# The end of a group of experts in another order: results copied ahead of the last roundings, the last subtraction in two halves, results and final squares piece by piece

## What is computed

```
g_w, g_idx = lax.top_k(g_prob, 1)                  # one of 8 groups for each token
top_v, top_i = lax.top_k(e_sel, TOP_K)             # two of the 8 experts of that group
gate = (g_w * jax.nn.softmax(top_v, axis=-1)).reshape(-1)
def expert_block(args):
    xb, e = args
    return (jax.nn.silu(xb @ w1[e]) * (xb @ w3[e])) @ w2[e]
x = x + hier_moe(h, ...)
return rms_norm(x, final_norm)
```

## Time and profile before

| | |
|---|---|
| median of 3 runs | 1842.92 us (1842.17 to 1843.37) |
| the profiled execution | 1841.25 us, its span 1839.4 us |
| busy TensorE matmuls | 1741.4 us (95%) |
| busy VectorE | 1521.0 us (83%) |
| busy ScalarE | 1219.1 us (66%) |
| busy GpSimd | 132.4 us (7%) |
| read from HBM | 542.33 MB, 295 GB/s over the span |
| loop over the groups | from about 890 us to 1825 us of the span |
| mean granted clock of TensorE | 0.991 |

### The profile page before, as it was taken

The page is one execution under the profiler, slowest core; times in us unless marked ns, Lnnn a source line. Parts: engine busy times, 40 slices in busy tenths (PEclk is TensorE's granted clock), DMA queues, the critical chain, the costliest instruction groups (busy, mean ns, idle before and its releaser), DMA issues.

```text
span 1839.4 us, 26378 instructions
## 1 busy us (share of the span) xinstructions
PE 1741.4 (95%) x10394; PEld 1522.0 (83%) x10394; DVE 1521.0 (83%) x1284; ACT 1219.1 (66%) x947; POOL 132.4 (7%) x140
## 2 busy tenths in 40 slices
PE   6999999999999999999999999999999999999996
PEld 6987899989899989978877877778777777778775
DVE  4787665678565666678899999999999999999997
ACT  4465444343323335545688988889898898888985
POOL 1155000000000001441000000000000000000000
PEclk9999999999999999999999999999999999999999
DMA  6431254563344555227699999999999999999994
GB/s 248 187 130 70 110 199 171 196 246 141 138 172 176 199 197 217 95 80 295 260 429 426 428 429 429 428 420 429 428 428 428 430 429 428 428 428 428 430 428 174
DMA packets 40645, 544.13 MB, mean 296 GB/s; under 512 B 4624, under 2 KB 4752, under 8 KB 5904
## 3 DMA queue, kind: packets, MB, share of 16 engines
q1 hardware_dynamic: 40592, 543.39, 72.1%
HBM read 542.33 MB, written 1.05 MB: 295 GB/s over the span
## 4 chain that ended last, share of the span: by engine, by line
PE 59%; DMA 13%; issue 7%; ACT 6%; DVE 4%; POOL 1%; DVEq 0%; ACTq 0%; POOLq 0%; SPq 0%
PE psum L1394 17%; DMA ring<-in_w 13%; PE psum L984 12%; PE psum L834 7%; PE psum L994 6%; PE psum L1408 4%; ACT arena_r L1802 4%; PE psum L1423 2%; DVE ring_r L2309 2%; PE psum L877 2%; PE psum L1159 1%; PE psum L894 1%; PE psum L1332 1%; PE psum L1296 1%; PE psum L1456 1%
## 5 line engine op out<-in xcount | busy, mean ns | idle before, releaser
L2309 DVE TENSOR_TENSOR ring_r<-ring,arena_r 128x4096 fp32r<-128x4096 f32 x192 | 846.7, 4418 | 17.1 <-ACT arena_r L1802 13.1
L1802 ACT ACTIVATE arena_r<-ring 128x4096 fp32r<-128x4096 f32 x188 | 682.3, 3629 | 65.6 <-DMA ring<-in_w 63.7
L1394 PE MATMUL psum<-arena_r,stream_r 128*128 128x512 f32 x1024 | 410.8, 401 | 11.5 <-DVE stream_r L2398 9.2
L1394 PE MATMUL psum<-ring_r,stream_r 128*128 128x512 f32 x1024 | 403.2, 394 | 0.0
L1394 PEld LDWEIGHTS psum<-arena_r,stream_r 128*128 128x128 f32 x1024 | 194.9, 190 | 56.5 <-DVE ring_r L2309 11.3
L1592 ACT ACTIVATE arena_r<-ring 128x3072 fp32r<-128x3072 f32 x40 | 110.9, 2773 | 188.6 <-DMA ring<-in_ffn 188.6
L1394 PEld LDWEIGHTS psum<-ring_r,stream_r 128*128 128x128 f32 x1024 | 194.9, 190 | 39.1
L984 PE MATMUL psum<-arena_r 128*128 128x256 f32 x672 | 190.2, 283 | 0.0
L984 PE MATMUL psum<-stream_r,ring_r 128*128 128x256 f32 x672 | 190.1, 283 | 0.0
L984 PE MATMUL psum<-stream_r,arena_r 128*128 128x256 f32 x672 | 190.1, 283 | 0.0
L1423 PE MATMUL psum<-arena_r 128*128 128x512 f32 x512 | 161.1, 396 | 11.7 <-DVE arena_r L2457 10.8
(11 more groups left out here) (327 smaller groups left out, 2675.8 us busy)
## 6 DMA issues: line engine op xcount, KB each, us to landing
ring<-in_w SPq DMA_DIRECT2D x192, 2048.0 KB, 12.9
ring<-in_ffn SPq DMA_DIRECT2D x44, 1536.0 KB, 6.3
ring<-in_w_in SPq DMA_DIRECT2D x8, 2048.0 KB, 8.1
ring<-in_in_w SPq DMA_DIRECT2D x7, 2048.0 KB, 13.0
ring<-in_out_w SPq DMA_DIRECT2D x7, 2048.0 KB, 8.2
ring<-in_l_in SPq DMA_DIRECT2D x8, 1536.0 KB, 8.5
ring<-in_proj SPq DMA_DIRECT2D x2, 2048.0 KB, 8.5
ring<-in_misc SPq DMA_DIRECT2D x1, 1632.0 KB, 8.8
```

What stands on the lines that cost most here:

```text
L1394: last = mm(dst, xg[:, k, :], b[:, k * D_EXPERT:(k + 1) * D_EXPERT], start=(k == 0 and b is u_hi), stop=(k == KD - 1 and b is u_lo))
L1802: A(w_hi[u % HI_SLOTS], ring[:, MOE_SLOT[at], :], ACT.Copy).then_inc(m_hi, 1)
L2309: V.tensor_tensor(ring_r[MOE_SLOT[u % NM]][:, :], raw, w_hi[u % HI_SLOTS].bitcast(F32), ALU.subtract).then_inc(m_lo, 1)
```

## The change

Seven edits; the counters keep their meaning where nothing else is said.

- ScalarE: the result copies of units 18 and 19 go ahead of the roundings H(21) and H(22), and from there on each rounding comes one iteration later. The new order: H(20), copy 17, copy 18, H(21), silu 6, copy 19, H(22), round 6, silu 7, H(23), round 7, H(24), gathered tokens, H(25), H(26), y, H(27).
- VectorE: L(23) is cut into two halves of 2048 columns. The new order: L(22), subtract 6, multiply 7, first half of L(23), subtract 7, second half, L(24), L(25), gathered tokens, L(26), y, L(27).
- TensorE starts unit 23 on the first half (`m_lo_first`) and waits for the second one in its middle.
- y: each half is counted by itself (`m_y_lo` goes by two per group), and `send_back` waits before each piece for the half that it reads.
- After the last group the step on rank stands in front of the last `add_back`.
- Each of the last two squares waits for the pieces of its own token half (`m_scd` starts at 2 instead of 1, and the waits on it are one higher).
- The copy of rank, `moe_done` and GpSimd's wait on it are gone.

```diff
@@ the plan of the units
+        LATE = MOE.index(("w1", PER_GROUP - 1)) - 1
@@ TensorE, expert_out
-                pe.wait_ge(m_lo, n * NM + (u + 1))
+                if u == NM - 1:
+                    pe.wait_ge(m_lo_first, n + 1)
+                else:
+                    pe.wait_ge(m_lo, n * NM + (u + 1))
...
                 for j in range(NE):
+                    if u == NM - 1 and j == NE // 2:
+                        pe.wait_ge(m_lo, n * NM + NM)
@@ TensorE, send_back
-                pe.wait_ge(m_y_lo, n)
                 for i, (tc, h) in enumerate(RES):
+                    pe.wait_ge(m_y_lo, 2 * n + h)
@@ ScalarE, the loop over the units
-                        if kind != "w2":
-                            act.wait_ge(m_unit, n * NM + (u + 1))
-                            A(h_raw[:, e % 2, 0 if kind == "w1" else 1, :], psum[:, H1_BANK if kind == "w1" else H3_BANK, :],
-                              ACT.Copy).then_inc(m_raw, 1)
+                        if kind != "w2" and u <= LATE:
+                            raw(u)
...
-                        if u + HI_SLOTS < NM:
-                            split_hi(u + HI_SLOTS, n)
-                        elif u < NM - 1:
-                            with act.If(n + 1 < passes * N_GROUPS):
-                                split_hi(u + HI_SLOTS, n)
+                        if u in (LATE, LATE + 1):
+                            raw(u + 1)
+                        if u < LATE + 2:
+                            next_hi(u + HI_SLOTS)
+                        elif u > LATE + 2:
+                            next_hi(u + HI_SLOTS - 1)
...
-            square("last", lambda tc: (moe_done, 1))
+            for tc in range(NT):
+                act.wait_ge(m_scd, passes * (4 * N_GROUPS) + 2 * tc)
+                A(xn[:, tc, :], x[:, tc, :], ACT.Square, accum_out=ss[:, NORMS["last"], tc:tc + 1]).then_inc(squares, 1)
@@ VectorE
+            def split_lo_rows(i, done):
+
+                slot, at = MOE_SLOT[NM - 1], slice(i * SLOT // 2, (i + 1) * SLOT // 2)
+                V.tensor_tensor(ring_r[slot][:, at], ring[:, slot, at], w_hi[(NM - 1) % HI_SLOTS][:, at].bitcast(F32),
+                                ALU.subtract).then_inc(done, 1)
...
-                        if u + 3 < NM:
+                        if u + 3 < NM - 1:
                             split_lo(u + 3, n)
-                        else:
-                            with dve.If(n + 1 < passes * N_GROUPS):
-                                split_lo(u + 3, n)
                         if u in FOLD_AT:
...
+                        if u + 3 == NM - 1:
+                            dve.wait_ge(m_hi, n * NM + NM)
+                            split_lo_rows(0, m_lo_first)
                         if u in TURN_AT:
...
+                        if u + 3 == NM:
+                            split_lo_rows(1, m_lo)
+                        if u + 3 >= NM:
+                            with dve.If(n + 1 < passes * N_GROUPS):
+                                split_lo(u + 3, n)
...
-                        last = V.tensor_tensor(y_lo[:, at], psum[:, Y_BANK[i], :], y_hi[:, at].bitcast(F32), ALU.subtract)
-                    last.then_inc(m_y_lo, 1)
+                        V.tensor_tensor(y_lo[:, at], psum[:, Y_BANK[i], :], y_hi[:, at].bitcast(F32),
+                                        ALU.subtract).then_inc(m_y_lo, 1)
                 n = dve.snap(p * N_GROUPS + N_GROUPS)
-                add_back(n)
                 V.tensor_scalar(rank, rank, float(CAP), None, ALU.subtract).then_inc(scaled_ready, 1)
                 dve.wait_ge(scaled_ready, p + (1 + NT))
-            dve.wait_ge(m_scd, passes * (4 * N_GROUPS) + 1)
-            V.tensor_copy(last_rank, rank).then_inc(moe_done, 1)
+                add_back(n)
```

More of the change, by code:

```diff
@@ L401, in program @@
         gate8, rank8, rank = few(NT, 8), few(NT, 8), few(NT)
-        last_rank, most, passes_f = few(NT), few(1), few(1)
+        most, passes_f = few(1), few(1)
         psum = ctx.enter_context(nc.psum_tensor("psum", [P, 8, 512], F32))
@@ L440, in program @@
         m_gate_mm, m_sel_turned, m_selT, m_gate = sem("m_gate_mm"), sem("m_sel_turned"), sem("m_selT"), sem("m_gate")
-        m_hi, m_lo, m_unit, m_silu, m_h = sem("m_hi"), sem("m_lo"), sem("m_unit"), sem("m_silu"), sem("m_h")
+        m_hi, m_lo, m_lo_first, m_unit, m_silu, m_h = sem("m_hi"), sem("m_lo"), sem("m_lo_first"), sem("m_unit"), sem("m_silu"), sem("m_h")
         m_raw, m_fold, m_hT_hi, m_hT_lo = sem("m_raw"), sem("m_fold"), sem("m_hT_hi"), sem("m_hT_lo")
         m_y_hi, m_y_lo, m_sc, m_scd = sem("m_y_hi"), sem("m_y_lo"), sem("m_sc"), sem("m_scd")
-        moe_done, out_ready, out_sent = sem("moe_done"), sem("out_ready"), sem("out_sent")
+        out_ready, out_sent = sem("out_ready"), sem("out_sent")
         O = PsumOrder(tile_ready, act_drained, dve_drained)
@@ L1414, in expert_out @@
                 e = MOE[u][1]
-                pe.wait_ge(m_lo, n * NM + (u + 1))
+                if u == NM - 1:
+                    pe.wait_ge(m_lo_first, n + 1)
+                else:
+                    pe.wait_ge(m_lo, n * NM + (u + 1))
                 pe.wait_ge(m_hT_lo, n * PER_GROUP + (e + 2))
                 if e == 0:
-                    pe.wait_ge(m_scd, n * 4 + 1)
+                    pe.wait_ge(m_scd, n * 4 + 2)
                 u_hi, u_lo = w_hi[u % HI_SLOTS], ring_r[MOE_SLOT[u]]
                 for j in range(NE):
+                    if u == NM - 1 and j == NE // 2:
+                        pe.wait_ge(m_lo, n * NM + NM)
                     for b in (u_hi, u_lo):
@@ L1814, in _, with raw, next_hi @@
                     n = act.snap(p * N_GROUPS + g)
+                    def raw(u):
+                        kind, e = MOE[u]
+                        act.wait_ge(m_unit, n * NM + (u + 1))
+                        A(h_raw[:, e % 2, 0 if kind == "w1" else 1, :], psum[:, H1_BANK if kind == "w1" else H3_BANK, :],
+                          ACT.Copy).then_inc(m_raw, 1)
+                    def next_hi(u):
+                        if u < NM:
+                            split_hi(u, n)
+                        else:
+                            with act.If(n + 1 < passes * N_GROUPS):
+                                split_hi(u, n)
                     for u, (kind, e) in enumerate(MOE):
-                        if kind != "w2":
-                            act.wait_ge(m_unit, n * NM + (u + 1))
-                            A(h_raw[:, e % 2, 0 if kind == "w1" else 1, :], psum[:, H1_BANK if kind == "w1" else H3_BANK, :],
-                              ACT.Copy).then_inc(m_raw, 1)
+                        if kind != "w2" and u <= LATE:
+                            raw(u)
                         if u in FOLD_AT:
@@ L1838, in _ @@
                         A(y_hi[:, i * 512:(i + 1) * 512], psum[:, Y_BANK[i], :], ACT.Copy).then_inc(m_y_hi, 1)
-                    with act.If(n + 1 < passes * N_GROUPS):
-                        split_hi(NM - 1 + HI_SLOTS, n)
+                    next_hi(NM - 1 + HI_SLOTS)
                 n = act.snap(p * N_GROUPS + N_GROUPS)
@@ L2356, in _ @@
             V.engine_nop().then_inc(r_gate, 1)
-            V.engine_nop().then_inc(m_scd, 1)
+            V.engine_nop().then_inc(m_scd, 2)
+            V.engine_nop().then_inc(m_y_lo, 1)
             V.engine_nop().then_inc(m_sc, 4)
@@ L2588, in _ @@
             norm(5)
-            pool.wait_ge(moe_done, 1)
             norm("last")
```

## The result

| | before | changed |
|---|---|---|
| median | 1843.14 us (1842.17 to 1845.72, 4 runs) | 1861.49 us (1856.75 to 1867.03, 4 runs) |
| the profiled execution | 1841.25, span 1839.4 | 1859.95, span 1858.1 |
| groups apart (start of unit 0 of the next group) | 117.7 | 120.85 |
| mean granted clock | 0.991 | 0.982 |

The changed kernel takes 1.0102 times as long, interval 1.0087 to 1.0116: slower, as forecast, by 18.4 us instead of 11. The time lies 7.5 us above the forecast and 1.5 above the range.

A forecast was written before the change was run, and what follows sets the result against it. The DMA was taken to set the pace, three resources lying within 6%. Seven passages x 2.1 = 14.7 us later landing puts unit 23's end 13.5 later; less 2.2 in the tail, +11.3: 1854 us, range 1841 to 1860.

The forecast's parts named there:

- the row with a like wait: TensorE at each next group's start: 1.8 us of slower matmuls after 7 us of standstill, chosen between 0 and 3.5.
- the tail: Behind the last group's unit 23: send-back, rank step and squares start earlier, a gain taken as 2.2 us.
- the slow GpSimd step: Inverse root behind the second square: 1.39 us beside a VectorE multiply, median 0.551; kept, else the tail would gain 2.8.
- Rival D: Passages: H(23) isn't late because fold 7 runs sooner; both gains stand, 1.2+2.2, faster at 1839.5 us; chance 0.08.
- Rival C: Passages: lateness is absorbed in each group, the stall staying below VectorE's spare 2.8 us; not slower, 1840.7 us; chance 0.17.
- the larger of the two: Passages: late loads' 2.1 us each exceeds VectorE's loss of 1.2 to 1.3 per group, so the loads count.
- the load lands 2.1 late: Unit 30's load, issued 5.95 us later against 3.8 slack, lands 2.1 late with all later ones, in each passage.
- M(19) starts about 1.0 after: TensorE: unit 19's matmuls start about 1.0 us after the end of L(19), VectorE's subtraction for that unit.
- Together 18.3: Chain from the end of unit 19's subtraction to that of L(23): 1.0 plus 17.3 us; VectorE is ready after 14.3.
- stall 4.0: VectorE's wait in each passage, 4.0 us, since its input takes 18.3 and it is ready after 14.3.
- the VectorE group of 118.8: VectorE's time per group, 114.7+0.1+4.0 us against the DMA's 117.5: 1.2 to 1.3 lost per group from the second passage.
- Rival B: Passages: the clock doesn't fall or loads keep their reserve, only VectorE's cycle counts: 1847 us (1845 to 1850); chance 0.25.

The follow-up runs named there:

- the half loads of before: The kernel before with each load bringing half the bytes, second half of each expert matrix left out: 1827.88 us, ratio 0.9902, groups 115.5 us apart.
- the filled kernel: The changed kernel with seven extra unused matmuls behind unit 23 of each group but the last, filling TensorE's standstill: 1854.04 us, ratio 1.0061.
- ScalarE's order undone: The changed kernel with copies and roundings on ScalarE in the order of before, VectorE's new order kept: 1853.88 us, ratio 1.0053.
- with the copies back: The changed kernel with seven extra matmuls per standstill, and result copies 18 and 19 back in their old places: 1854.31 us, ratio 1.0052.
- half loads of the changed kernel: The changed kernel with each load bringing half the bytes, second half of each expert matrix left out: 1854.66 us, ratio 1.0049.

## Why the prediction was right in kind and short in size

**Right, by its own steps.** H(23) stands behind silu 7, which waits for fold 7 behind the gather: 5.03 us idle, predicted 5.02 late. Unit 0 of the second group starts at 1012.12, 4.19 later than before (predicted 4.15). TensorE idle 7.2 (7.0). Slow matmuls 1.9 us per passage (1.8); the choice of the row with a like wait out of the ends 0 and 3.5 held. In the first passage the load of unit 30 landed 2.2 late (2.1); the timeline of SP's queue has its issue, and the DMA view of that microsecond the time to its landing, 7.6 us:

```profile
1018.24 0.33 SPq L739 DMA_DIRECT2D ring<-in_w  x1
```
```profile
ring<-in_w SPq DMA_DIRECT2D x1, 2048.0 KB, 7.6
```

Unit 23 gained 1.4 (1.2), the tail 2.2 (2.2); the slow GpSimd step that the tail was to keep is there, though it is another one (1.07 and 0.55 us for the last two, before 0.19 and 1.39). Rival D fell with silu 7's wait of 5.03. Rival C fell too: the waits of VectorE make 4.87 per passage and its reserve is 2.8, which the half loads of before confirm. And "the larger of the two, so it is the one that counts" held: H(20) starts at its landing, so the cycle through the loads is the longer one in all passages but the last.

**The step that failed** is the size of that larger term: "the load lands 2.1 late, all later ones behind it too", "2.1 us per passage". H(20) of the last group starts 22.3 us later than before, 3.2 for each passage (2.3 to 4.9) instead of 2.1; 22.3 less the predicted 14.7 is 7.6, and the forecast was short by 7.5. The cycle through the loads, part by part, as the prediction's rows give it and as the six full cycles of the changed kernel show it on the mean:

| part of the cycle, us | predicted | measured |
|---|---|---|
| start of unit 0 to the issue of unit 30's load | 5.92 | 6.10 |
| issue to landing | 7.6 | 7.66 |
| 14 more landings, to that of unit 20 | 68.55 | 69.19 |
| that landing, H(20), to unit 0 of the next group | 37.55 | 37.90 |
| sum | 119.6 | 120.85 |

Half of the error is in the third line. The prediction lets all later loads follow at 4.9 us each and adds nothing. In the trace one or two of them come late once more behind every passage, 5.1 to 5.7 us after the one before: 0.4 to 1.2 us each time. The rest is the fall of the clock inside a group that the prediction charges to no passage (1.57 us, once, in the second), 0.2 us on the mean in the first line, and less than 0.1 us in the second and in each of the other chains.

The distances between the groups show two cycles, of which the longer one counts each time:

| passage | 1 | 2 | 3 | 4 | 5 | 6 |
|---|---|---|---|---|---|---|
| units 0 and 1 behind it, us | 9.57 | 9.70 | 9.07 | 10.40 | 9.54 | 9.06 |
| from there to the next passage, us | 122.58 | 120.87 | 120.00 | 121.29 | 120.50 | 119.86 |

Where the clock costs least (the sixth), the distance is that of VectorE's cycle, 119.9; where it costs more, the loads are the later ones and the distance grows with it. The first has the 1.57 on top, and the later loads lost most there (1.15). With the clock held, the same parts give the loads 118.6 (4.1 for the first, 37.6 for the last): less than VectorE's 119.88, and so the filled kernel has that.

**A second step was wrong and didn't decide the sum:** "M(19) starts about 1.0 after" the end of L(19). It starts 2.1 after. The prediction adds up M(18) and fold 6 with the waits of the kernel before, where fold 6 waited 0.22. With VectorE late in every group, multiply 5, round 5, H(20) and copy 17 are late too, and fold 6 waits for that copy. "Together 18.3" is 19.5, "stall 4.0" is 4.86, and the VectorE group of 118.8 is 119.88: 2.4 lost per group, not 1.2 to 1.3. Rival B rested on that cycle: its 1847 with the true term (6 x 1.1 more) is 1853.6, and the filled kernel, which is this case, took 1854.04. In the changed kernel it is only the floor that the last distance meets. It was luck that this error had no weight: at 2.4 it is larger than the 2.1 that the prediction held against it.

**An omission** with no effect on the sum: only ScalarE's queue was named as the carrier. The run with its order undone shows that multiply 7 ahead of L(23) on VectorE carries a loss as well (1.0053).

**Open.** Why one or two of the later loads lose time again is not known: they land 8 to 9.5 us after their issue, near the 7.4 to 7.9 of an emptied queue, and no run took this apart. The four runs of the changed kernel spread over 10 us, those of before over 3.6 (7.7 in the 20 runs beside the first experiments), those of the filled kernel over 1.3, with the copies back over 3.9. That the unfilled standstills, with a clock that falls more in one passage than in another, make part of the spread is likely by this, but only argued; another part lies ahead of the loop, whose first unit starts between 891.6 and 898.1 us in the traces.

## What to carry to other kernels

Before a step is put ahead of another one in an in-order queue, look up when its input comes in the steady loop, not in the last turn: here the same order gains 1.4 us once where the gather is absent and costs some 3 us in each of seven passages where it is present. When a loop has two or three engines within a few per cent of its bound, a stall has to be followed once around the whole cycle with the engines already late, since waits that are zero now (a fold for a copy, a rounding for a multiply) open up; and where two cycles close over the same chain, the longer one counts in each turn, so both have to be sized with all their parts: here each was 1.1 to 1.2 us short in 120. A load that lands late can be followed by others that lose time again (5.1 to 5.7 us instead of 4.9). Often the repair is not to undo the order but to move what makes its input late.

## What the runs showed of the hardware

- A standstill of TensorE of 5.3 to 7.2 us between matmuls of 128x512 in f32 was followed by slower matmuls in all 21 passages of three runs (changed kernel, ScalarE's order undone, half loads of the changed kernel): 8.9 to 10.5 us for two units instead of 7.54, with a granted clock of 0.55 over the first 4 us where it was read. After 3.2 us it happened in five passages of seven, after 1.1 to 1.3 us in none of these places; but once a wait of 0.97 us in front of unit 19 was followed by a clock of 0.72 over 4 us. The Trainium skill (TensorE: Matmul & The Clock Gate, HAM oscillation) describes this restart after every wait, and the trace agrees for the long ones. What it cost was decided elsewhere: nothing with half loads, 1 us with full ones.
- Seven matmuls in the standstill of each of seven passages made the changed kernel some 7 us faster (ratios 1.0061 against 1.0102), with no useful work in them.
- A load of 2 MB takes 7.4 to 7.9 us from issue to landing when the queue has run empty (seven passages of the changed kernel), against a landing every 4.9 us in a full one. When the issue comes later than that before the next landing is due, the DMA stands still in between: the dips of the page.
